# Three layers on one core: the first three feature tiles after each block boundary in two halves of the tokens

## The reference

```python
for i in range(DEPTH):                       # DEPTH = 2
    m = _even_mixer(...) if i % 2 == 0 else _odd_mixer(...)
    x = _layer_norm(DN_ALPHA * x + m, ln1_g[i], ln1_b[i])
    x = _layer_norm(DN_ALPHA * x + _sq_relu_mlp(x, w_up[i], w_down[i]), ln2_g[i], ln2_b[i])
    gate = jax.nn.sigmoid(x @ ple_w_gate[i] + ple_b_gate[i])
    x = x + gate * (p[i] @ ple_w_proj[i])
# then second_block
h = rmsnorm(x, norm1_g); x = x + mixed(h @ w_in) @ w_out
h2 = rmsnorm(x, norm2_g); x = x + (silu(h2 @ w_ffn_gate) * (h2 @ w_ffn_up)) @ w_ffn_down
return rmsnorm(x, norm_f_g)
```

## Time and profile before

| | us |
|---|---|
| median of 3 runs | 1978.52 |
| the profiled execution | 1976.43 |
| its span | 1974.6 |
| outside the span | 1.8 |
| PE busy | 1945.5 (99%) |
| POOL busy | 1261.2 (64%) |
| DVE busy | 871.2 (44%) |
| ACT busy | 327.1 (17%) |

### The profile page before, as it was taken

The page is one execution under the profiler, slowest core; times in us unless marked ns, Lnnn a source line. Parts: engine busy times, 40 slices in busy tenths (PEclk is TensorE's granted clock), DMA queues, the critical chain, the costliest instruction groups (busy, mean ns, idle before and its releaser), DMA issues.

```text
span 1974.6 us, 24552 instructions
## 1 busy us (share of the span) xinstructions
PE 1945.5 (99%) x9180; PEld 1614.1 (82%) x9180; DVE 871.2 (44%) x1208; ACT 327.1 (17%) x627; POOL 1261.2 (64%) x818
## 2 busy tenths in 40 slices
PE   9999999999999999999999999999999999999998
PEld 8788788888887878888788888877888788888886
DVE  3587372253349511472832343377457840000234
ACT  1376300000003100461300000033122130000001
POOL 5586576667767547775566677756553556666674
PEclk9999999999999999999999999999999999999999
DMA  6311233333332323112233332322222233333332
GB/s 228 128 33 33 85 107 96 96 96 117 96 96 85 97 76 107 55 53 85 67 126 96 96 117 96 96 86 86 68 86 65 75 96 97 96 96 96 96 96 75
DMA packets 53698, 181.31 MB, mean 92 GB/s; under 512 B 6584, under 2 KB 9322, under 8 KB 53498
## 3 DMA queue, kind: packets, MB, share of 16 engines
q1 hardware_dynamic: 46656, 165.17, 26.6%
q10 hardware_dynamic: 6970, 15.11, 2.2%
HBM read 176.56 MB, written 3.70 MB: 91 GB/s over the span
## 4 chain that ended last, share of the span: by engine, by line
PE 90%; DVE 4%; POOL 3%; ACT 1%; issue 1%; POOLq 0%; DVEq 0%
PE PS L643 87%; POOL WL L532 1%; PE PS L812 1%; PE PS L891 1%; POOL WH L529 1%; POOL PB L560 1%; DVE PS L1585 0%; DVE X L1602 0%; DVE STL L1868 0%; ACT HT L2104 0%; DVE U L1930 0%; DVE STH L1867 0%; DVE ST L1877 0%; ACT PTH L2055 0%; DVE PTL L1515 0%
## 5 line engine op out<-in xcount | busy, mean ns | idle before, releaser
L532 POOL TENSOR_TENSOR WL<-RW,WH 128x1024 fp32r<-128x1024 f32 x301 | 762.5, 2533 | 25.1
L529 POOL TENSOR_SCALAR WH<-RW 128x1024 fp32r<-128x1024 f32 x301 | 352.0, 1169 | 626.3 <-PE PS L643 602.2
L643 PE MATMUL PS<-XTH,WH 128*128 128x512 f32 x1168 | 456.9, 391 | 2.1 <-DVE XTL L1635 1.6
L643 PE MATMUL PS<-XTL,WH 128*128 128x512 f32 x1168 | 454.8, 389 | 0.0
L643 PE MATMUL PS<-XTH,WL 128*128 128x512 f32 x1168 | 454.6, 389 | 0.0
L643 PE MATMUL PS<-WL,HSH 128*128 128x512 f32 x688 | 267.5, 390 | 2.1 <-POOL WL L532 2.1
L643 PE MATMUL PS<-WH,HSL 128*128 128x512 f32 x688 | 267.7, 389 | 0.0
L643 PE MATMUL PS<-WH,HSH 128*128 128x512 f32 x688 | 267.7, 389 | 0.0
L643 PEld LDWEIGHTS PS<-XTH,WH 128*128 128x128 f32 x1168 | 219.2, 188 | 50.8 <-DVE XTL L1635 3.7
L643 PEld LDWEIGHTS PS<-XTH,WL 128*128 128x128 f32 x1168 | 219.2, 188 | 46.1
L643 PEld LDWEIGHTS PS<-XTL,WH 128*128 128x128 f32 x1168 | 219.3, 188 | 43.9
(11 more groups left out here) (337 smaller groups left out, 2306.0 us busy)
## 6 DMA issues: line engine op xcount, KB each, us to landing
RW<-stream SPq DMA_DIRECT2D x302, 512.0 KB, 3.6
BC<-gate_rows SPq DMA_DIRECT2D x16, 256.0 KB, 3.1
G<-gain_rows ACTq DMA_DIRECT2D x5, 512.0 KB, 3.5
X<-x ACTq DMA_DIRECT2D x1, 2048.0 KB, 12.4
G<-bias_vecs ACTq DMA_DIRECT2D x4, 512.0 KB, 5.1
out<-X SPq DMA_DIRECT2D x4, 512.0 KB, 2.7
XS<-xt ACTq DMA_DIRECT2D x3, 512.0 KB, 8.7
bias_rows<-QM ACTq DMA_DIRECT2D x1, 1536.0 KB, 6.8
```

What stands on the lines that cost most here:

```text
L529: pool.tensor_scalar(WH[:, j % WS, :], RW[:, j % RAW, :], 1.0, 1.0, ALU.mult, ALU.mult).then_inc(hi_split, 1)
L532: pool.tensor_tensor(WL[:, j % WS, :], RW[:, j % RAW, :], WH[:, j % WS, :].bitcast(F32), ALU.subtract).then_inc(lo_split, 1)
L643: return pe.matmul(o, a, b, start=start, stop=stop)
```

## The change

It touches only the boundaries and what stands beside them.

- DVE splits the first three feature tiles (`SPLIT_K = 3`) in two halves of 256 tokens. The first half is split as soon as the first two token tiles are copied, and before the fourth token tile is scaled. ACT applies gains to halves of tiles 1 and 2 in the same way.
- PE (`first_group`) multiplies the halves: tiles 0 and 1 of the first half, with the transposes of the fourth token tile between or behind, tile 2, and then the three second halves, each product with 256 columns. Since half a bank is begun at a time, the four banks are first set to zero by a multiplication with a tile of zeros (`clear`), and all products accumulate. In the embedding stages `gate_half` orders the same halves by its token tiles, with whole matmuls.
- POOL makes the high part of the second chunk after each boundary, but waits with its low part until the third tile's first half is split (the wait on `ready_parts`).
- ACT loads the table of the square root ahead of the first, fourth and sixth boundary (an activation on `SPARE`).
- At the third and sixth boundary the transposed tiles use four banks in turn (`t % 2 + 2`), `occupy` is called less often, and in the sums of the forget gates the four products of 512 columns become products of 512, 384, 256 and 128.

```diff
+SPLIT_K = 3
+HALVES = (slice(0, S // 2), slice(S // 2, S))
+def ready_parts(b, k, half):
+    base = KD + (KD + SPLIT_K) * b
+    return base + (half * SPLIT_K + k + 1 if k < SPLIT_K else SPLIT_K + k + 1)
...
-            return (t if BOUND[b][0] else (t + 2) % T) * D
+            return (t if BOUND[b][0] else t % 2 + 2) * D
...
                 pool.wait_ge(hi_split, 2 * (j + 1) + 2 * RAW * i)
+                if b is not None:
+                    pool.wait_ge(xt_ready, ready_parts(b, SPLIT_K - 1, 0))
                 pool.tensor_tensor(WL[:, j % WS, :], RW[:, j % RAW, :], WH[:, j % WS, :].bitcast(F32),
...
+            cut_stages(FIRST["out0"] + WS - 1, ((0, "up0"), (1, "ple0"), (2, "fox")), c + 3)
...
+            def first_group(c, b, turn_tile):
+                def one(k, half):
+                    u, cc = UNIT * (k % 2), c + k // 2
+                    ts = slice(0, S) if half is None else HALVES[half]
+                    pe.wait_ge(xt_ready, ready_parts(b, k, half or 0))
+                    for m in range(4):
+                        w = slice(u + m * P, u + (m + 1) * P)
+                        x = mm3(PS[:, m, ts], WH[:, cc % WS, w], WL[:, cc % WS, w],
+                                XTH[:, k, ts], XTL[:, k, ts], False, k == KD - 1)
+                    return x
+                chunk(c)
+                one(0, 0)
+                if not BOUND[b][0]:
+                    turn_tile(T - 1)
+                one(1, 0)
+                if BOUND[b][0]:
+                    turn_tile(T - 1)
+                chunk(c + 1)
+                one(2, 0)
+                one(0, 1)
+                one(1, 1).then_inc(chunk_used, 1)
+                one(2, 1)
+                for k in range(SPLIT_K, KD):
...
+                if add:
+                    pe.wait_ge(yt_copied, 5 * b + 1)
+                    occupy(0, 3)
+                elif not kind:
+                    pe.wait_ge(y_ready, Y_BASE[b] + T)
+                clear(0)
+                clear(1)
+                if add:
+                    pe.wait_ge(yt_copied, 5 * b + 2)
+                clear(2)
+                clear(3)
+                turn_tile(b, 2)
+                first_group(c, b, lambda t: turn_tile(b, t))
...
+                    for half in range(2):
+                        if half:
+                            pe.wait_ge(yt_copied, 5 * b + 5)
+                        for k in range(SPLIT_K):
...
+                            pe.wait_ge(xt_ready, ready_parts(b, k, half))
+                            for t in (2 * half, 2 * half + 1):
+                                x = one(k, t)
...
-                    mm(PS[0:RANK, 4, :], LF[:, RANK * t:RANK * (t + 1)],
-                       STEPS[:, 3 * P - t * P:3 * P - t * P + S], t == 0, t == T - 1)
+                    mm(PS[0:RANK, 4, t * P:], LF[:, RANK * t:RANK * (t + 1)],
+                       STEPS[:, 3 * P:3 * P + S - t * P], t == 0, t == T - 1)
...
+                    split_half(0, 0)
+                    split_half(1, 0)
+                    split_half(2, 0)
+                    if kind and add:
+                        scale(3)
+                    for k in range(SPLIT_K):
+                        split_half(k, 1)
...
+                if kind and b in (0, 3, 5):
+                    act.activation(SPARE[:, 0:1], EPS[:, 0:1], F.Sqrt)
```

More of the change, by code:

```diff
@@ L660, in chunk, with features @@
                     pe.wait_ge(lo_split, c + 1 + r)
-            def features(c, bank, r=0, new=0, freed=None, late=None, steps=None):
+            def first_group(c, b, turn_tile):
[21 more added lines that the diff above has]
+                for k in range(SPLIT_K, KD):
+                    if k % 2 == 0:
+                        chunk(c + k // 2)
+                    x = one(k, None)
+                    if k % 2:
+                        x.then_inc(chunk_used, 1)
+            def features(c, bank, r=0, freed=None, steps=None):
                 columns, k_tiles = (0, P, 2 * P, 3 * P), KD
@@ L859, in attend, with turn_tile, boundary @@
                 pv(last)
-            def boundary(b, embed=None):
+            def turn_tile(b, t):
+                add, kind, n = BOUND[b]
+                if kind and t < T - 1:
+                    pe.wait_ge(centred, 3 * n + t + 1)
+                elif kind:
+                    pe.wait_ge(last_centred, n + 1)
+                else:
+                    pe.wait_ge(y_ready, Y_BASE[b] + t + 1)
+                if not add and t == 0:
+                    pe.wait_ge(emb_z, 16 if kind else 8)
+                elif not add and t >= 2:
+                    pe.wait_ge(yt_copied, 5 * b + t - 1)
+                src = YN[:, t, :] if kind == "rms" else X[:, t, :]
+                for k in range(KD):
+                    o = turned_at(b, t) + P * k
+                    x = pe.transpose(PSF[:, o:o + P], src[:, k * P:(k + 1) * P], IDENT[:, :])
+                x.then_inc(x_turned, 1)
+            def boundary(b, c, embed=None):
                 add, kind, n = BOUND[b]
@@ L867, in boundary @@
                     occupy(4, 8)
[L868 to L895, removed]
+                    pe.wait_ge(var_ready, 4 * n + T)
+                    occupy(0, 5)
+                turn_tile(b, 0)
+                turn_tile(b, 1)
                 if embed:
+                    pe.wait_ge(yt_copied, 5 * b + 1)
+                    embed(0)
                     embed(1)
+                    turn_tile(b, 2)
                     pe.wait_ge(yt_copied, 5 * b + 2)
@@ L988, in gate_half, with embedding @@
                     x.then_inc(*((gate_summed, 1) if t < T - 1 else (chunk_used, 1)))
[L990 to L993 removed]
+            def embedding(c, layer, b):
+                gate_half(c + 1, b)
                 gate_half(c + 5, freed=8 * layer)
@@ L1222, in _ @@
             block_end(3, "out1", "up1", "down1", 8, 8, 32, 32)
-            boundary(4, lambda t: embed_tile(FIRST["ple1"], 1, 0, t))
-            embedding(FIRST["ple1"], 1, 6)
-            boundary(5)
+            boundary(4, FIRST["ple1"], lambda t: embed_tile(FIRST["ple1"], 1, 0, t))
+            embedding(FIRST["ple1"], 1, 4)
             c = FIRST["gla"]
-            features(c, 0, new=7, late=30)
+            boundary(5, c)
             def low_rank(_):
@@ new lines, in split @@
+                def split(k, ts=slice(0, S)):
+                    y = YT[:, k, ts]
+                    if k == 0 and layer:
+                        own(ve.tensor_scalar(y, y, GAINS[:, n, 0:1], BIASES[:, n, 0:1], M, A))
+                    elif k == 0 and kind:
+                        own(ve.tensor_scalar(y, y, GAINS[:, n, 0:1], None, M))
+                    own(ve.tensor_copy(XTH[:, k, ts], y))
+                    ve.tensor_tensor(XTL[:, k, ts], y, XTH[:, k, ts].bitcast(F32), SUB).then_inc(xt_ready, 1)
@@ new lines, in split_half @@
+                def split_half(k, half):
+                    if k and kind:
+                        ve.wait_ge(yt_ready, (KD + SPLIT_K - 2) * n + (SPLIT_K - 1) * half + k)
+                    else:
+                        ve.wait_ge(yt_copied, 5 * b + 2 + 2 * half)
+                    split(k, HALVES[half])
+                if kind:
+                    residual(0)
+                    residual(1)
+                    if add:
+                        scale(0)
+                    residual(2)
+                    if add:
+                        scale(1)
+                    residual(3)
+                    if add:
+                        scale(2)
+                    if b == 7 or not add:
+                        scale(3)
```

153 lines of the change are left out of this document (80 added, 73 removed).

## The result

The changed kernel takes 1983.32 us (median of 9 runs, 1981.94 to 1985.8), the kernel before 1978.88 beside it (9 runs). The ratio is 1.0025, interval 1.0016 to 1.0034: 4.4 us slower, where 14.6 faster was forecast. Profile to profile it is 1983.15 for 1976.43, 6.7 us; that is what has to be explained here.

What follows compares the result with a forecast made beforehand. PE, busy 99% of the span, bounds the kernel. 6.2 + 5.3 + 1.0 + 0.6 + 0.4 + 1.3 - 0.2 = 14.6 us gain, from 1976.43 to 1961.8, plus 2.1 for the median: 1963.9; 8 in 10 between 1959 and 1974.

Steps and rivals of the forecast that it cites:

- Elsewhere: Outside the boundaries: Pool's extra loops fall in idle time and a later-freed slot's load is covered by three other slots.
- the 0.2 for a second memset: At the opening: a second memset ahead of the first matmul costs 0.2 us.
- Second and fifth boundary: Embedding stages: resources tight, DVE at the gate sums by 625 to 628; gain 0.5 us each, bounds gain 1.3, loss 2.5.
- Rival (a): DVE comes late in both embedding stages: -2.5 us each for +0.5, total 1969.9 us; chance 0.2.
- Rival (d): Gaps at boundaries lower PE's clock, doubling the first group's 8.6 us; with three such boundaries 1989.7 us; chance 0.04.
- First, fourth, sixth boundary, forget sums: Gains of 3.1 us each at first and fourth boundary, 5.3 at the sixth, 1.3 in the gate sums.
- Rival (b): Held low part collides with fourth scaling and second halves, 2 us at each of four layer-norm boundaries: 1971.9 us; chance 0.07.
- (c): Rival: the halves bring nothing, as PE waits for second chunk or second half instead: 1973.5 us; chance 0.08.
- The preload's part: First, fourth and sixth boundary: loading ACT's table early takes its 1.28 us from between squares and root.
- The hold: Sixth boundary: holding Pool's low part spares the DVE scaling its wait of 1.56 us.
- Seventh: Seventh boundary: POOL's low part wins over the fourth scaling, which ends at 1606.3; gain 0.4 us (-1 to 1.5).
- Third: Third boundary, where only copies and splits stand: gain 0.6 us (0 to 1.2).

Runs made afterwards that it cites:

- spare_wide: The changed kernel with SPARE 64 wide in place of 32, so HSH begins on a multiple of 256 bytes: 1971.84 us, ratio 0.9965.
- place_before: The kernel before with ZERO and SPARE allocated where the changed kernel has them, used by nothing: 1990.67 us, ratio 1.0064.
- hs_shift: The kernel before with 640 bytes left free ahead of HSH, moving only HSH, HSL and GT: 1991.31 us, ratio 1.0067.
- place_after: The changed kernel with ZERO and SPARE allocated above all others, so every other tile keeps its old address: 1971.67 us, ratio 0.9969.
- turn_early: The changed kernel with the fourth token tile's transposes ahead of the fourth embedding product at the second and fifth boundary: 1977.9 us, ratio 0.9997.
- no_hold: The kernel with the edits of place_after and turn_early, with Pool's low part of the second chunk started at once at every boundary: 1978.41 us, ratio 1.0003.
- no_preload: The kernel with the edits of place_after and turn_early, without the three early square roots that load ACT's table: 1969.03 us, ratio 0.9956.
- hold7: Against both: Pool's low part at the seventh boundary waits for the fourth scaling; linear attention tiles moved to multiples of 256 bytes: 1963.83 us, ratio 0.9924.
- both: The changed kernel with the edits of place_after and turn_early together: 1966.42 us, ratio 0.9936.
- hs_128: The kernel before with 128 bytes left free ahead of HSH: 1989.79 us, ratio 1.0054.
- hs_32: The kernel before with 32 bytes left free ahead of HSH: 1991.91 us, ratio 1.0062.
- xt_shift: The kernel before with 128 bytes free ahead of XTH and behind XTL, so these two alone begin off 256: 2004.32 us, ratio 1.0127.

## Why the prediction was wrong

- **The sum has no term for the memory that the change takes.** The step is "Elsewhere", which looks at Pool's loops and a slot's load only. The diff's two sb() lines move HSH and HSL off a multiple of 256 bytes: 11.1 us, the largest single effect of the change. Of the 640 bytes SPARE's 128 do it; with SPARE at 256 (spare_wide) the loss is gone. No row of the trace before gives its size, since there both operands of all long stages lie on such multiples; but the 0.227 a product of the earlier trace rows was taken over as if it held wherever the tiles lie, and what the two allocations move was neither priced nor bounded (the 0.2 for a second memset is the time to fill ZERO, not its place). Shown by place_before, hs_shift and place_after.
- **"Second and fifth boundary: I take 0.5, near the upper end since the work in all is the same."** The place was right (PE waiting for a gate bank, DVE late), and so was the step before it: DVE was to begin its second halves at 604.5, and less the 2.1 by which the kernel is late there it began at 604.7. The end of DVE's row was forecast at 625 to 628 and came at 628.7 by the same clock (630.77 less 2.1). I took the upper end for a reason that doesn't bear on it: with DVE as with PE it isn't the work that counts but the idle 3.3 us ahead of it and what Pool holds meanwhile. Rival (a), chance 0.2, is what happened, at -3.2 or so per boundary for its -2.5. Shown by turn_early. How the 3.2 divides, place_after shows: the same wait of 3.06 cost 1.5 at its second boundary, where the clock stayed at 1.00, and 3.2 at its fifth, where it fell.
- **Rival (d) was asked at the wrong place.** "The longest gap in my schedule is 1.4 us" held at the boundaries that lead into `features`: their longest gap is 1.21 us, and the first one's group runs at the full clock (239 to 250 us, granted clock 1.00). But the wait of rival (a) is 3.06 us long and itself brings the clock down: some eight products at 0.43 for 0.227, 1.6 us more at each of the two. The two rivals were priced as if apart, and the one sets off the other. The Trainium skill, "TensorE: Matmul & The Clock Gate", section "What's actually happening", has the clock fall after an idle stretch; the traces agree in three of four waits of this length (in place_after the fifth boundary's is followed by a granted clock of 0.64 from 1338.0 to 1341.6 us, the second's by 1.00). In no_hold waits of 2.13 and 2.16 us (first and fourth boundary) brought it down and one of 2.66 (seventh) did not, nor did one of 2.19 in the kernel before (sixth). So the length of the wait alone did not decide it; what else did, no run here shows.
- **First, fourth, sixth boundary, forget sums: right.** 2.7, 3.2, 4.5 and 1.3 us for 3.1, 3.1, 5.3 and 1.3. Rival (b) did not come: the fourth scaling at the first boundary takes 1.35 (from 240.90) with Pool's low part beside it (2.38 from 240.94). Nor did (c). The halves start 0.12 apart, as taken from the earlier trace rows. The preload's part was right (no_preload: 1.3, 1.3 and 1.0).
- **The hold was under-priced.** The prediction prices it at the sixth alone, 1.6 us. no_hold shows 12 us over seven boundaries, part of it through the clock: at the first one Pool would start its low part just as DVE begins to split, and there the operation shut out goes from SBUF to SBUF. My sum held only because the held version was what it worked out. The Trainium skill, "SBUF — State Buffer", section "SBUF: two separate sides", says that whoever starts first keeps the shared pair for the whole instruction. Here the trace agrees, 2.42 for 0.40 behind a low part that began 0.08 earlier. At the seventh boundary it does not: by the profile the scaling began 0.05 ahead of Pool, and it was the scaling that took 2.98 for 0.75, while Pool's 2.38 is its normal time. Starts so close don't tell who was first.
- **Seventh: off by 1.0, though the lock was right.** The loss of 0.6 for a gain of 0.4 is inside the stated -1 to 1.5. "POOL wins: scaling to 1606.3" came true: it ended at 1610.01, and less the 3.5 by which the kernel is late there that is 1606.5. What was too short came behind it. The third tile ended 0.6 later than the forecast's 1613.3 (1617.4 less 3.5), since the second halves began late, and then PE waited 0.3 us for Pool's third chunk (it starts at 1620.50, 0.54 behind the product ahead of it), for which the seventh's sum has no term. hold7 takes Pool's low part behind the scaling and gains 1.4 there.
- **Third: 0.6 forecast, about 0 measured** (0.1 to 0.2 in both); its lower bound was 0.
- **The chances.** "Faster 0.88 (forecast, (a), (b) and half of (c))": these parts add up to 0.92. It changes nothing in the argument.
- **Opening.** +0.55 for +0.2, but it was -0.05, +0.62 and +1.22 in the profiles of place_after, hold7 and both, which begin alike. Those are the same instructions with a spread of 1.3 us between executions, so the forecast's 0.2 is neither borne out nor refuted.

## What to carry to other kernels

A tile's start is part of its cost. When a diff allocates anything, add up what lies ahead of each matmul operand and see that it still begins on a multiple of 256 bytes; 128 bytes of scratch cost this kernel 11.7 us, more than all its boundary work brought (7.1, by place_after). Where a first half of work is pulled forward, ask what its second half now waits for on another engine's row, and price that wait with the clock it may cost PE, not by the sum of the work. And compare two traces first by a regular event of the whole run, such as the start of every chunk: it gives the balance of each stage to 0.1 us, where the median tells 2.

## What the runs showed of the hardware

- A matmul of 512 columns on float32 parts started every 0.2267 us with both operands on multiples of 256 bytes, every 0.2324 us with the stationary one 128 or 640 bytes off or the moving one 128 off, and every 0.2333 us with the stationary one 32 bytes off, at a granted clock of 1.00 in all and with no wait shown (means of the distances of starts, before, after, hs_shift, hs_128, hs_32 and xt_shift). Other offsets and the products of 128 and 256 columns were not timed alone.
- The Trainium skill, "SBUF — State Buffer", section "Operand start alignment", asks only for a multiple of the element's size, and says of itself that it speaks of what is legal and that nothing was timed; the runs here add the time.
- The same wait of 3.06 us brought PE's granted clock down three times (after twice, place_after once) and left it once.
